# A hybrid SSD and sparse-attention step: 523 steps in another order, the scan's last state first, other places for copies and loads

## What is computed

```python
gate, z_s, xbc, dt_raw, q, kv_c, kv_s, kv_w, g_raw, z_a = layer_inputs(x, c, pos, w_ada, b_ada, norm_g, w_in)
y_ssd, conv_new, ssm_new = ssd_branch(z_s, xbc, dt_raw, conv0, h0, ...)   # chunked scan, SiLU(z) gate, norm
o = nsa_prompt(q, kv_c, kv_s, kv_w)     # or nsa_sample: pages are gathered by a page table
x = layer_output(x, gate, y_ssd, o, g_raw, z_a, att_norm_g, w_out)
y = rms_norm(x, final_g)
```

## Time and profile before

| | |
|---|---|
| median of 3 runs | 866.78 us (865.96 to 870.12) |
| profiled execution | 873.36 us, span 871.5 us |
| TensorE busy | 825.4 us, 95% of the span |
| VectorE, ScalarE, GpSimd busy | 524.8, 359.0 and 263.4 us |
| mean granted TensorE clock | 0.984 |
| DMA | 89.04 MB, mean 102 GB/s |

### The profile page before, as it was taken

The page is one execution under the profiler, slowest core; times in us unless marked ns, Lnnn a source line. Parts: engine busy times, 40 slices in busy tenths (PEclk is TensorE's granted clock), DMA queues, the critical chain, the costliest instruction groups (busy, mean ns, idle before and its releaser), DMA issues. The chain is left out here.

```text
span 871.5 us, 20078 instructions
## 1 busy us (share of the span) xinstructions
PE 825.4 (95%) x8505; PEld 539.8 (62%) x8505; DVE 524.8 (60%) x1095; ACT 359.0 (41%) x739; POOL 263.4 (30%) x232
## 2 busy tenths in 40 slices
PE   3999999999999999999999999798999999999997
PEld 2447998877788766567555555555456565655563
DVE  2146553376789744556544536867878778776632
ACT  4041002011212255446334236854766656465623
POOL 2047888370000043235310110429401230301121
PEclk9899999999999999999999999989999999999999
DMA  9963165553220000300943550920102001112102
GB/s 300 336 208 106 49 191 207 237 193 114 80 75 1 24 6 1 95 3 1 354 148 119 175 175 7 262 72 8 44 15 87 2 28 50 28 51 74 62 3 97
DMA packets 45410, 89.04 MB, mean 102 GB/s; under 512 B 4388, under 2 KB 26076, under 8 KB 43210
## 3 DMA queue, kind: packets, MB, share of 16 engines
q1 hardware_dynamic: 38202, 54.94, 19.9%
q0 software_dynamic: 6080, 31.79, 10.5%
q10 hardware_dynamic: 1040, 1.05, 0.4%
HBM read 75.49 MB, written 16.40 MB: 105 GB/s over the span
## 5 line engine op out<-in xcount | busy, mean ns | idle before, releaser
L2204 PE MATMUL PS<-W,hT 128*128 128x512 f32 x256 | 113.0, 594 | 0.3 <-DVE W L1823 0.3
L1988 DVE CUSTOM_DVE_ANT_0 PS<-PS,consts 128x640 f32<-128x640 f32 (+5 forms) x96 | 77.4, 835 | 30.9 <-PE PS L2623 30.6
L2204 PEld LDWEIGHTS PS<-W,hT 128*128 128x128 f32 x256 | 47.9, 190 | 56.0 <-issue 54.8
L1105 POOL TENSOR_TENSOR Q<-Q,U 128x512 f32<-128x512 f32 x16 | 20.5, 1280 | 163.8 <-DVE U L2025 139.4
L1435 ACT ACTIVATE hT<-PS,small 128x128 f32<-128x128 f32 (+7 forms) x64 | 47.0, 740 | 49.0 <-DVE small L1988 47.7
L2590 PE MATMUL PS<-U,Y 128*128 128x512 f32 x128 | 60.2, 603 | 0.0
L2590 PE MATMUL PS<-U,Q 128*128 128x512 f32 x128 | 59.1, 598 | 0.0
L1435 ACT ACTIVATE T<-PS,small 128x640 f32<-128x640 f32 (+4 forms) x64 | 41.8, 667 | 22.7 <-DVE small L1988 21.6
L2004 DVE STREAM_TRANSPOSE hT<-hT 128x1024 f32<-128x1024 f32 (+6 forms) x29 | 42.8, 1488 | 1.3 <-ACT hT L1435 1.3
L2590 PEld LDWEIGHTS PS<-U,Q 128*128 128x128 f32 x128 | 23.5, 190 | 29.0 <-issue 28.9
L2623 PE MATMUL PS<-KTsw,W 64*128 64x512 f32 (+3 forms) x128 | 39.4, 517 | 0.3 <-ACT KcTs L1427 0.2
(11 more groups left out here) (545 smaller groups left out, 1845.5 us busy)
## 6 DMA issues: line engine op xcount, KB each, us to landing
W<-in_w_in SPq DMA_DIRECT2D x4, 2048.0 KB, 8.0
W<-in_w_ada SPq DMA_DIRECT2D x7, 1024.0 KB, 16.3
U<-in_x_prompt SPq DMA_DIRECT2D x8, 512.0 KB, 11.5
W<-in_w_ada SPq DMA_DIRECT2D x2, 2048.0 KB
U<-in_state_win_kv POOLq DMA_DIRECT2D x8, 512.0 KB
W<-in_x_prompt SPq DMA_DIRECT2D x8, 512.0 KB, 3.4
out_y_prompt<-W SPq DMA_DIRECT2D x8, 512.0 KB, 2.6
out_new_win_sample<-in_state_win_kv POOLq DMA_DIRECT2D x1, 4032.0 KB, 24.5
```

What stands on the lines that cost most here:

```text
L1105: nc.gpsimd.tensor_tensor(Q3[:, i, :], Q3[:, i, :], spare, ALU.add).then_inc(s_added, 1)
L1988: ins = nc.vector.tensor_tensor_reduce(x, x, strip(u), 1.0, -NEG, ALU.add, ALU.min, sneg_m[u % 2][:, m:m + 1])
L2204: ins = nc.tensor.matmul(bank(z_bank(u)), hT3[:, k, i * P:(i + 1) * P], w, start=(k == 0), stop=(k == KT8 - 1))
```

## The change

Six things, all of order; no operation is added or taken away but one wait of SP.

1. `ORDER` is another string of the same 523 letters (it differs from the first hundred steps on).
2. The end of the scan on VectorE: for chunk 7 the product and the sum that make the last `hst` come ahead of the rows of Y, and signal `s_hTs_dve`. The two bank copies, `hlast` and the two products `Bblk`, which stood at the head of chunk 8, now stand in chunk 7 between its diagonal part and its last sum, which is the one that counts `s_ssd_y` up to 8.
3. TensorE transposes the stored states in another order, and waits for `s_hTs_dve` where it waited for `s_ssd_y` to be 8; `ssd_B(8)` doesn't wait for `s_ssd_y` any more.
4. `queries_dve(0)` stands ahead of VectorE's copies of the turned probabilities in the last round.
5. SP waits in rounds 1 to 3 for the round's second page gather before it issues the value loads.
6. The waits of the steps follow from the string.

```diff
-        NAT = (0, 1, 2, 3, 4, 6, 5, 7)
+        NAT = (0, 1, 2, 3, 4, 7, 6, 5)
@@ ORDER (begins; 523 letters each)
-            "qqxsxyxssmwsvctxszqtxyksxtvscsxtkgxsmxcwvvasyxkwusmtgtxtspxoapptoorropoooxpctossxtvvkuptsxpcsvvvxsqx"
+            "qsqxxsyxzmsctxwsvsqtxkxysctxvmskwsgstxxcvvssayxmwukttqsxxgootoporrxoptotocoaptsvvsxpkpuxxststtvcvxvx"
...
@@ vector engine, scan
-                if i == TT:
-                    for n in (6, 7):
-                        dve.wait_ge(s_natT, n + 1)
-                        nc.vector.tensor_copy(hTs[:, NAT[n], :], bank(NAT[n])).then_inc(s_hTs_dve, 1)
-                    dve.wait_ge(s_natT, NB + 1)
-                    nc.vector.tensor_copy(hlast, bank(0)).then_inc(s_hout, 1)
-                    for g, d in enumerate(Bblk):
...
+                if i == TT - 1:
+                    dve.wait_ge(s_chunk_done, TT)
+                    link(nc.vector.tensor_tensor(heads(hst), heads(hst), over_d(chunk_decay[i]), ALU.mult))
+                    nc.vector.tensor_tensor(hst[:, :], hst[:, :], bank(7), ALU.add).then_inc(s_hTs_dve, 1)
...
                 nc.vector.tensor_tensor(y, heads(bank(5), r), heads(sk[i % 2], r), ALU.add).then_inc(s_ydiag, 1)
+                if i == TT - 1:
+                    for n in (6, 7):
+                        dve.wait_ge(s_natT, n + 1)
+                        nc.vector.tensor_copy(hTs[:, NAT[n], :], bank(NAT[n])).then_inc(s_hTs_dve, 1)
+                    dve.wait_ge(s_natT, NB + 1)
+                    nc.vector.tensor_copy(hlast, bank(0)).then_inc(s_hout, 1)
+                    for g, d in enumerate(Bblk):
...
                 dve.wait_ge(s_ydiag, i + 1)
                 if i:
                     ins = nc.vector.tensor_tensor(y, y, heads(yo, r), ALU.add)
-                if i < TT:
+                if i < TT - 1:
...
                 ins.then_inc(s_ssd_y, 1)
@@ vector engine, rounds
+                if p == NB // 2 - 1:
+                    queries_dve(0)
                 dve.wait_ge(s_turned, 10 * p + 8)
...
-                if p == NB // 2 - 1:
-                    queries_dve(0)
@@ tensor engine
-                if i:
+                if i == 0:
+                    pe.wait_ge(s_taps, 2)
+                elif i < TT:
                     pe.wait_ge(s_ssd_y, i)
...
-                    pe.wait_ge(s_hTs_dve, 2)
+                    pe.wait_ge(s_hTs_dve, 3)
...
                 if b == 7:
-                    pe.wait_ge(s_ssd_y, 8)
+                    pe.wait_ge(s_hTs_dve, 1)
...
-            pe.wait_ge(s_ssd_y, 8)
+            pe.wait_ge(s_hTs_dve, 1)
@@ sync engine
             for p in range(NB // 2):
+                if p:
+                    sp.wait_ge(s_pages[1], PAGES_IN[1] + 16 * (p + 1))
                 for k in "sw":
                     load_values(sp, k, p)
```

More of the change, by code:

```diff
@@ L734, in build_layer @@
         ORDER = (
-            "qqxsxyxssmwsvctxszqtxyksxtvscsxtkgxsmxcwvvasyxkwusmtgtxtspxoapptoorropoooxpctossxtvvkuptsxpcsvvvxsqx"
[L736 to L740, removed]
+            "qsqxxsyxzmsctxwsvsqtxkxysctxvmskwsgstxxcvvssayxmwukttqsxxgootoporrxoptotocoaptsvvsxpkpuxxststtvcvxvx"
+            "xtpssopxpqktsnsoxxtogtscsroootoorsvxvnvafkstvsvxyvvscxmutwgxxtsooossxaokqxorsyxuxostsxoosnstrxvvxstx"
+            "vsttcsxvwxmkssvxxxsxtsxxvvscsvttfxxvsyxkqgotssmtowxxtssoorrxnoxoxxootsvasvsscvvssvxxtkuxfxsxxsvsvsxs"
+            "tvxcxvssvvxsygtxoassttwxoofxksosmsuotorqxotxrxtxostcvvsvvvsksvnxxvxxsxxsvvssvssxcvtxtgvtsktxrxoaooox"
+            "svxsxsxvvttcxfssyvvxssouookonxoorwsmgsttrxoxofoorsotxoxsvxsvssxvavsbxbxsvvtndudtvctvovvokoovcvvhorfk"
+            "goooarnohuorfonoorhooof")
         VALUE_TILES = [min(u // 2, WIN // P if u % 2 else TT) + 1 for u in range(2 * TT)]
@@ L1788, in _ @@
                     dve.wait_ge(s_conv_stored, 32)
-                if i == TT:
-                    for n in (6, 7):
-                        dve.wait_ge(s_natT, n + 1)
-                        nc.vector.tensor_copy(hTs[:, NAT[n], :], bank(NAT[n])).then_inc(s_hTs_dve, 1)
-                    dve.wait_ge(s_natT, NB + 1)
-                    nc.vector.tensor_copy(hlast, bank(0)).then_inc(s_hout, 1)
-                    for g, d in enumerate(Bblk):
-                        nc.vector.tensor_tensor(d.rearrange("p (b n) -> p b n", b=4), Btok[0][0:SR, g * P:(g + 1) * P].unsqueeze(1).broadcast_to([SR, 4, P]),
-                                                const("ind4")[0:SR].unsqueeze(2).broadcast_to([SR, 4, P]), ALU.mult).then_inc(s_Bblk, 1)
+                if i == TT - 1:
+                    dve.wait_ge(s_chunk_done, TT)
+                    link(nc.vector.tensor_tensor(heads(hst), heads(hst), over_d(chunk_decay[i]), ALU.mult))
+                    nc.vector.tensor_tensor(hst[:, :], hst[:, :], bank(7), ALU.add).then_inc(s_hTs_dve, 1)
                 dve.wait_ge(s_chunk_done, i + 1)
@@ L1807, in _ @@
                 nc.vector.tensor_tensor(y, heads(bank(5), r), heads(sk[i % 2], r), ALU.add).then_inc(s_ydiag, 1)
+                if i == TT - 1:
[5 more added lines that the diff above has]
+                    for g, d in enumerate(Bblk):
+                        nc.vector.tensor_tensor(d.rearrange("p (b n) -> p b n", b=4), Btok[0][0:SR, g * P:(g + 1) * P].unsqueeze(1).broadcast_to([SR, 4, P]),
+                                                const("ind4")[0:SR].unsqueeze(2).broadcast_to([SR, 4, P]), ALU.mult).then_inc(s_Bblk, 1)
                 dve.wait_ge(s_ydiag, i + 1)
@@ L2376, in ssd_B @@
                 r = rows(i)
-                if i:
+                if i == 0:
+                    pe.wait_ge(s_taps, 2)
+                elif i < TT:
                     pe.wait_ge(s_ssd_y, i)
-                else:
-                    pe.wait_ge(s_taps, 2)
                 if 0 < i < TT:
```

## The result

On one chip, 12 runs of each kernel: 869.75 us median before (865.96 to 874.66), 874.0 us changed (871.3 to 881.31). The ratio is 1.0065, 95% interval 1.0040 to 1.0091: slower, a little over the 0.5% that I had set as the limit of what can be told. A second set of runs gave 1.0103 (1.0058 to 1.0149, six runs of the changed kernel). The forecast was 874, range 862 to 880, slower. The number came out; the way to it did not. Part of that is luck with the base: I had added 7.2 us to 866.78, the median of three runs of the kernel before, and twelve runs put it at 869.75. The medians differ by 4.25 us, by the ratio it is 5.7.

What follows compares the result with a forecast made beforehand. TensorE, busy 825 of 871.5 us, was taken as the bound, plus its waits and low clock. Terms +10.6 +2.9 -1.2 -1.1 -4.0 = +7.2 us took the median from 866.78 to 874, range 862 to 880.

Steps and rivals of the forecast that it cites:

- The load late by VectorE's chain: End of the scan: `s_ssd_y` = 8, and with it the gate weights' issue, moves from 413.79 to about 416.9 us.
- How long it then takes: Second gate's weights: sharing the DMA engines, they land at about 433.5 us; `z_unit(9)` starts 10.6 us later.
- rival 1: Gate weights late by VectorE's chain alone, keeping 9.0 us from issue: +3.0 there, -2.3 in all, 864.5 us; chance 0.30.
- The rule of sharing: DMA queues 0 and 1: packets go nearly one to one; weights get 0.137 MB/us beside 4 KB packets, 0.09 beside gathers.
- The cold clock: TensorE after its idle wait for the gate weights: clock at 1.2 GHz, costing 2.9 us (1 to 4).
- Gather and queries: Rounds: value loads behind page gathers give -1.2 us in round 2; queries copied ahead give -1.1 at round 3's end.
- The steps' order: Steps from 539 us on: the new order shortens TensorE's waits, -4 us (-1 to -8).
- The counter-example that I gave: Scan's end, GpSimd contention: second product `Bblk` (L1796, 0.67 us) also reads SBUF twice and was not slowed.
- The low clock of 561 to 579 us: Steps: TensorE's clock, granted at 0.72 there, more likely than not stays low after the change.
- the likeliest case: Gate weights share the DMA queues and `z_unit(9)` starts 10.6 us late: 874 us (868 to 880); chance 0.60.
- rival 3: Steps: the order is worth more or less, low clock gone (another -4) or back elsewhere (+3); no separate chance.

Runs made afterwards that it cites:

- The experiment with the later issue: The changed kernel, but SP waits for `s_ssd_y` = 9, one sum later than 8, before loading the second gate's weights: 890.32 us (one run).

## Why the forecast was right in number and half right in its reasons

- **The load late by VectorE's chain.** Right: issue at 416.10, as a wait that nobody had moved now stood behind five more instructions. I had put it at 416.9, with 3.07 us for the chain. It was 2.24 in the profiles, as L1791 took 1.05 us and the load's chain began 0.33 us earlier.
- **How long it then takes: the step that failed** is what the load gets before queue 0 sends. Forecast: first packets 2 us after the issue, alone from 418.9 to 420.9 us, 0.75 MB, and 1.35 MB left to share. Measured: first packets 1 us after the issue (50 in 417 to 418 us, nearly the full rate from 418), alone until 422, 1.65 MB, and 0.45 MB left. The rule of sharing, one packet to one and 0.14 MB/us beside 4 KB packets, held; it had a third of the work. Used from 426.13, not 433.5; the term was +3.2, not +10.6. In size this was rival 1 (+3.0), to which I gave 0.30, but not by its rule: of the 3.2 us the issue makes 2.24, and 1.0 is the sharing. The experiment with the later issue shows the forecast's mechanism at full size, at 2.4 us more.
- **Why queue 0 sent so late** stays open. Its first transfer, the 256 KB store, was issued at 417.90 and its first packets lie in 421 to 422 us; in the kernel before the times are 418.23 and 420 to 421. In the kernel with the later load they are 417.21 and 418 to 419, and there the load was issued only at 418.46.
- **The cold clock.** Forecast +2.9, measured 5.2 - 3.2 = +2.0.
- **Gather and queries.** -1.2 and -1.1, both as measured.
- **The steps' order: wrong in sign.** Forecast -4.0. In this pair of traces it gained 2.7 to the first output product and lost 6.5 behind it, so +3.8. The gain did not repeat: from the first step to the first output product the changed kernel took 36.2 us and 39.2 in its second trace, the old order 35.5 to 38.3. The loss did: the steps took 336.1 and 338.9 us, the old order's 324.4 to 331.6, and the kernel before has the longest of these, so that this pair shows too little of it. I laid the letters over the old durations, and two durations changed: 0.42 us became 2.81 and 6.00, as L1983 met GpSimd's products. I had cited the contention for L1812 and did not ask of each two-input instruction of VectorE in the new order what GpSimd does at that time; the earlier trace rows had the price, and the hold of L2019 (2.52 us) stood in the same trace. The counter-example that I gave, L1796 with 0.67 us, was none: GpSimd's row of products had ended at 415.42, before it began. The wait near 750 no row of before announced.
- **The low clock of 561 to 579 us** left in the profiled execution (I had kept it) and came back at 605 to 612 and 755 to 759, behind the two new waits. In the second trace it was there, from 573 to 580, as well.

So 3.2 + 2.0 - 1.2 - 1.1 + 3.8 = +6.7 (6.5 in the span): +7.2 forecast from errors of -8.3 us in two terms and +7.8 in the third. That they cancel is luck, and so is the base. By the mechanism, the load was late in the likeliest case's way and by rival 1's amount, and rival 3 came true with its sign turned against me.

## What to carry to other kernels

When a block is moved on one engine, look at who counts on its semaphores' old place: here a load waited for a sum that it did not need, and a wait for the last true reader of its buffer (`s_ydiag`), took the ratio from 1.0065 to 1.0013, and with the old order from 1.0016 to 0.9939. When steps are reordered, lay GpSimd's busy stretches beside every VectorE instruction with two inputs in SBUF; durations do not move along with the letters. And where two queues share the DMA engines, count first how much each moves while it is alone, microsecond by microsecond: the share was the same all through, and the time hung on where queue 0's first packets lay.

## What the runs showed of the hardware

- VectorE's subtraction of 128x256 with both inputs in SBUF (0.42 us alone) waited past four boundaries between GpSimd's products of some 1.23 us (from 600.59 to the end of the last product at 606.31), and took 1.14 us in the kernel before with the new order. The Trainium skill (SBUF — State Buffer, SBUF: two separate sides) calls the shared port an exclusive lock that is held for the whole instruction, the other blocking fully. That agrees for each single product; the hold across a row of them is longer than one instruction.
- The same 2 MB on queue 1 took 9.0, 10.0 and 17.25 us from issue to use, as it was issued 5.4 and 2.65 us before the window loads and 0.4 us after them. The Trainium skill (DMA: Bandwidth & Descriptors, Queues, rings and completion order) has the engines go round the queues packet by packet. By the profile's packets this agrees wherever both queues send: 211 to 190 and 265 to 252 beside window loads, 182 to 172 and 179 to 183 beside gathers. What queue 1 then moves follows from the other's packets: 0.14 MB/us beside 4 KB, 0.09 beside 8 KB rows, 0.40 alone.
- The clock of a stretch is not the kernel's alone: from 540 to 579 us the changed kernel ran at full clock in one execution and at a mean of 0.92 in another, 0.87 with the load behind `s_ydiag`. What a gain ahead of such a stretch is worth can't be read from one trace.
